# Seven block products of 256 columns in place of eight for twelve gate and up tile pairs of each layer

## The reference

```python
g_, u_ = jnp.split(h @ w_gate_up[i], 2, axis=-1)      # h: 512 x 1024, w_gate_up: 1024 x 5632
h2 = layer_norm(DEEPNORM_ALPHA * h + (jax.nn.silu(g_) * u_) @ w_down[i], ln2_g[i], ln2_b[i])
```

## Time and profile before

| | |
|---|---|
| median of three runs | 2374.94 us |
| the profiled execution | 2375.34 us |
| its span, first to last instruction | 2373.7 us |
| PE busy | 2340.2 us, 99% of the span |
| DVE, ACT, POOL busy | 1463.1, 1356.0, 460.5 us |
| moved by DMA | 402.79 MB, mean 170 GB/s |

### The profile page before, as it was taken

The page is one execution under the profiler, slowest core; times in us unless marked ns, Lnnn a source line. Parts: engine busy times, 40 slices in busy tenths (PEclk is TensorE's granted clock), DMA queues, the critical chain, the costliest instruction groups (busy, mean ns, idle before and its releaser), DMA issues.

```text
span 2373.7 us, 34430 instructions
## 1 busy us (share of the span) xinstructions
PE 2340.2 (99%) x11448; PEld 1936.3 (82%) x11448; DVE 1463.1 (62%) x2572; ACT 1356.0 (57%) x2239; POOL 460.5 (19%) x557
## 2 busy tenths in 40 slices
PE   8999999999999999999999999999999999999999
PEld 6878888887777888888788888888878778888886
DVE  4899898989545211113758999989895461111147
ACT  5756657376564554344757566664755655544446
POOL 2222222222111111111112122221211111111110
PEclk9999999999999999999999999999999999999999
DMA  7676575857888788888675857747578887888985
GB/s 206 142 168 152 124 175 120 185 127 162 181 180 201 167 194 191 192 209 187 162 157 121 184 127 162 175 109 171 132 176 179 185 187 179 192 191 196 213 186 139
DMA packets 112251, 402.79 MB, mean 170 GB/s; under 512 B 12400, under 2 KB 12400, under 8 KB 112112
## 3 DMA queue, kind: packets, MB, share of 16 engines
q0 software_dynamic: 54144, 195.06, 48.1%
q1 hardware_dynamic: 55728, 200.56, 26.1%
q10 hardware_dynamic: 2240, 5.42, 0.6%
HBM read 398.89 MB, written 2.10 MB: 169 GB/s over the span
## 4 chain that ended last, share of the span: by engine, by line
PE 81%; ACT 8%; DVE 6%; DMA 3%; issue 2%; DVEq 0%; SPq 0%; POOLq 0%; ACTq 0%
PE bank L882 22%; PE bank L884 22%; PE bank L883 22%; PE bank L924 3%; PE bank L925 3%; PE bank L927 3%; DMA w_lo<-w_stream 2%; ACT decay L515 2%; PE bank L1001 1%; ACT w_lo L464 1%; ACT w_hi L463 1%; PE bank L1007 1%; PE bank L1221 1%; DVE tmp_m L1403 1%; ACT y_hi L536 1%
## 5 line engine op out<-in xcount | busy, mean ns | idle before, releaser
L882 PE MATMUL bank<-x_hi,w_hi 128*128 128x512 f32 x1728 | 686.0, 397 | 0.1
L884 PE MATMUL bank<-x_hi,w_lo 128*128 128x512 f32 x1728 | 673.4, 390 | 0.0
L883 PE MATMUL bank<-x_lo,w_hi 128*128 128x512 f32 x1728 | 672.7, 389 | 0.0
L362 POOL DMA_DIRECT2D w_lo<-w_stream x376 | 323.3, 860 | 1654.7 <-ACT w_lo L464 1574.9
L463 ACT ACTIVATE w_hi<-w_raw 128x1024 fp32r<-128x1024 f32 (+1 forms) x378 | 400.3, 1059 | 281.5 <-PE bank L884 240.0
L464 ACT ACTIVATE w_lo<-w_raw 128x1024 fp32r<-128x1024 f32 (+1 forms) x378 | 397.6, 1052 | 0.0
L882 PEld LDWEIGHTS bank<-x_hi,w_hi 128*128 128x128 f32 x1728 | 324.6, 188 | 69.0 <-issue 3.7
L884 PEld LDWEIGHTS bank<-x_hi,w_lo 128*128 128x128 f32 x1728 | 324.4, 188 | 68.5
L883 PEld LDWEIGHTS bank<-x_lo,w_hi 128*128 128x128 f32 x1728 | 324.7, 188 | 68.0 <-issue 3.4
L1316 DVE SCALAR_TENSOR_TENSOR z_a<-glu_out,params,z_a 128x497 f32<-128x497 f32 (+14 forms) x480 | 320.8, 744 | 0.0
L1794 DVE TENSOR_TENSOR glu_out<-bank,sigmoids 128x512 f32<-128x512 f32 x44 | 30.4, 692 | 405.0 <-PE bank L884 405.0
(11 more groups left out here) (256 smaller groups left out, 3564.4 us busy)
## 6 DMA issues: line engine op xcount, KB each, us to landing
w_raw<-w_stream SPq DMA_DIRECT2D x362, 512.0 KB, 5.1
w_lo<-w_stream POOLq DMA_DIRECT2D x360, 512.0 KB, 7.7
w_raw<-w_stream SPq DMA_DIRECT2D x16, 384.0 KB, 3.7
w_lo<-w_stream POOLq DMA_DIRECT2D x16, 384.0 KB, 5.9
z_b<-x_in SPq DMA_DIRECT2D x4, 512.0 KB, 7.6
out<-z_b SPq DMA_DIRECT2D x4, 512.0 KB, 6.2
ple_p<-p_in ACTq DMA_DIRECT2D x2, 512.0 KB, 6.6
w_ple_in<-w_ple ACTq DMA_DIRECT2D x2, 512.0 KB, 12.4
```

The costliest lines, as they stand in the source:

```text
L362: gp.dma_start(wlo[:, s, 0:n], w_stream[cyc, s, :, 0:n].bitcast(F32R), accum_op=ALU.add).then_inc(lo_done[s], 16)
L882: pe.matmul(dst, wh, mh, start=first, stop=False)
L883: pe.matmul(dst, wh, ml, start=False, stop=False)
L884: return pe.matmul(dst, wl, mh, start=False, stop=last)
```

## The change

The first 4 of the 16 pairs of `C_UP0` and `C_UP1` stay as they were (`WHOLE`, two cycles). The other 12 of each layer become "units". In a unit the gate tile and the up tile are one 2x2 block matrix (rows: gate, up; columns: the lower and the upper half of the input features), and `h` is a 2x2 block matrix too (the two halves of the features by the two halves of the tokens). The product of the two has eight block products; the change forms it with seven (`P1` to `P7`) from sums and differences of blocks:

- four combinations of `h` (`combine`), made once per layer from `z_a` with its bias, split in high (ACT, `combined_hi`) and low (DVE, `combined_low`), each 128x1024;
- four combinations of the weights of each unit (`sums`: `S1` to `S4`, 128x512 each, on DVE), rounded by ACT (`sum_hi`), with the low part by DVE (`sum_low`);
- three products with plain weight blocks (`P1`, `P2`, `P4`), rounded by ACT from the staged tiles (`ringed`) and completed by POOL's adding DMA, 256 KB each, in a ring of four half slots;
- each product is 4 x 3 = 12 matmuls of 128x256 into one half bank; DVE puts the four output blocks together with seven additions of 256 columns (`out`, `finish`), ACT keeps `P1` and applies Silu to the gate in two halves.

The staged tiles of a unit come by two loads of 512 KB to `z_a` or `w_raw`, three units in turn. `z_a` is overwritten, so DVE adds `x_hi` and `x_lo` again behind the last unit. The additions of the bias to `z_a` move on ACT ahead of the first tile of the part. The core of the diff:

```diff
+RING_ORDER = [(0, "P1"), (0, "P2"), (0, "P4"), (1, "P1")]
+for _n in range(UNITS):
+    RING_ORDER += [(_n + 1, "P2"), (_n + 1, "P4"), (_n + 2, "P1")]
+RING_ORDER = [(_n, _p) for _n, _p in RING_ORDER if _n < UNITS]
...
+                for n in range(UNITS):
+                    j = n % STAGES
+                    if n >= STAGES:
+                        sp.wait_ge(s_sum, seen(4 * (UNITS * L + n - STAGES) + 4))
+                        sp.wait_ge(ring_done, seen(RINGED * L + ringed_until(n - STAGES, "P4")))
+                    elif j == 1:
+                        for s in (2, 3):
+                            sp.wait_ge(hi_done[s], seen(L * CYCLES + C_DOWN0))
+                    else:
+                        sp.wait_ge(t_done, seen(4 * (L + 1)))
+                    for t in range(2):
+                        w = w_units[L * UNITS + n, t]
+                        if j == 1:
...
-                for first, end, n in ((C_GATE_A, C_DOWN2, WT), (C_DOWN2, C_PLE, LAST * P), (C_PLE, CYCLES, WT)):
+                for first, end, n in ((C_GATE_A, C_DOWN0, WT), (C_DOWN0, C_DOWN2, WT), (C_DOWN2, C_PLE, LAST * P), (C_PLE, CYCLES, WT)):
+                    if first == C_DOWN0:
+                        for i, (u_, p) in enumerate(RING_ORDER):
+                            q = ring_place(u_, p) % SLOTS
+                            gp.wait_ge(ring_done, seen(RINGED * L + i + 1))
+                            settle(gp)
+                            t, h = {"P1": (1, 0), "P2": (1, 1), "P4": (0, 1)}[p]
+                            gp.dma_start(part(wlo, q), w_units[L * UNITS + u_, t, :, h * HALF:(h + 1) * HALF].bitcast(F32R),
+                                         accum_op=ALU.add).then_inc(ring_lo[q], 16)
                     with gp.Fori(first + (first == C_GATE_A), end) as c:
                         lo(base + c, 0, 1, 2, 3, n=n)
...
+                for m in range(KT):
+                    act.wait_ge(xl_done, seen(KT * k + m + 1))
+                    act.activation(za[:, m, :], za[:, m, :], ACT.Identity,
+                                   bias=par[:, O_LN1 + KT + m:O_LN1 + KT + m + 1]).then_inc(zf_ready, 1)
...
+                    j, c = n % STAGES, ring_place(n, p)
+                    act.wait_ge(unit_loaded[j][0 if p == "P4" else 1], 16 * (UNITS // STAGES * L + n // STAGES + 1))
+                    if c >= SLOTS:
+                        after(*ring_owner(c - SLOTS))
+                    w = staged(n, {"P1": 2, "P2": 3, "P4": 1}[p])
+                    act.activation(part(whi, c % SLOTS), w, ACT.Copy)
+                    act.activation(part(wlo, c % SLOTS), w, ACT.Copy, scale=-1.0).then_inc(ring_done, 1)
+
...
+                def frame(n):
+
+                    if n > 0:
+                        gate_columns(n - 1, 1, g2_done)
+                    if n < UNITS:
+                        sum_hi(n, "S4")
+                        after(n, "P1")
+                        act.wait_ge(fl_done, seen(FT * L + WHOLE + n - 1))
+                        act.activation(u[:, n % 2, 0:HT], bank[product_bank(n, "P1")][:, 0:HT], ACT.Copy).then_inc(kept, 1)
+                        if n < UNITS - 1:
+                            ringed(n + 1, "P2")
+                            ringed(n + 1, "P4")
+                        else:
+                            hi(on(post, C_DOWN0), 0)
+                        sum_hi(n, "S3")
+                    if n > 0:
+                        unit_hi(n - 1)
+                    if n < UNITS:
+                        gate_columns(n, 0, g1_done)
+                        ringed(n + 2, "P1")
+                    if n < UNITS - 1:
+                        sum_hi(n + 1, "S1")
+                        sum_hi(n + 1, "S2")
+                    elif n == UNITS - 1:
+                        after(n, "P4")
+                        hi(on(post, C_DOWN0), 1)
+                        after(n, "P5")
+                        hi(on(post, C_DOWN0), 2)
+                        after(n, "P7")
+                        hi(on(post, C_DOWN0), 3)
+
+                for i in range(4):
+                    combined_hi(i)
+                for f in range(WHOLE):
+                    r = f % 2
+                    c = on(post, C_UP0 + f // 2)
+                    last = f >= WHOLE - 2
+                    take(c, 2 * r, sg[:, :], ACT.Silu)
+                    if not last:
+                        hi(on(c, 1), 2 * r)
+                    elif r == 1:
+                        sum_hi(0, "S1")
+                        sum_hi(0, "S2")
+                    act.wait_ge(evac[2 * r + 1], seen(c[1] + 1))
+                    act.activation(aah[:, f, :], u[:, r, :], ACT.Copy).then_inc(fh_done, 1)
+                    if not last:
+                        hi(on(c, 1), 2 * r + 1)
+                    elif r == 0:
+                        ringed(0, "P1")
+                        ringed(0, "P2")
+                        ringed(0, "P4")
...
+                for n in range(UNITS + 1):
+                    frame(n)
...
-                swiglu(on(post, C_UP0), KT, aah)
-                for m in range(KT):
-                    act.wait_ge(xl_done, seen(KT * k + m + 1))
-                    act.activation(za[:, m, :], za[:, m, :], ACT.Identity,
-                                   bias=par[:, O_LN1 + KT + m:O_LN1 + KT + m + 1]).then_inc(zf_ready, 1)
-                swiglu(on(post, C_UP1), KT, abh)
...
+                        mh, ml = xh[:, a:a + 4, t:t + HT], xl[:, a:a + 4, t:t + HT]
+                    else:
+                        i = {"P5": 0, "P6": 1, "P7": 2, "P4": 3}[p]
+                        mh, ml = combined(i, 0), combined(i, 1)
+                    wh, wl = part(whi, q), part(wlo, q)
+                    for k_ in range(4):
+                        w = slice(k_ * P, (k_ + 1) * P)
+                        i = three(bank[product_bank(n, p)][:, 0:HT], wh[:, w], wl[:, w], mh[:, k_, :], ml[:, k_, :],
+                                  k_ == 0, k_ == 3)
...
+                for n in range(UNITS):
+                    for p in ORDER:
+                        product(n, p)
...
                 dve.wait_ge(zf_ready, seen(2 * KT * (L + 1)))
-                settle(dve)
+                combine(0, quadrant(0, 1), quadrant(0, 0))
+                dve.wait_ge(t_ready, seen(4 * L + 1))
+                combine(1, quadrant(1, 1), combined_sum(0))
+                combine(2, quadrant(1, 1), quadrant(0, 1))
+                dve.wait_ge(t_ready, seen(4 * L + 2))
+                combine(3, quadrant(1, 0), combined_sum(1))
+                for i in range(4):
+                    combined_low(i)
...
+                            for t in range(2):
+                                dve.wait_ge(unit_loaded[n % STAGES][t], 16 * (UNITS // STAGES * L + n // STAGES + 1))
+                            a, b, op = staged(n, 0), staged(n, 1), ALU.add
+                        elif name == "S2":
+                            dve.wait_ge(s_sum, seen(count + 1))
+                            a, b, op = part(wsum, S_BUF["S1"]), staged(n, 2), ALU.subtract
+                        elif name == "S4":
+                            dve.wait_ge(s_sum, seen(count + 2))
+                            a, b, op = staged(n, 3), part(wsum, S_BUF["S2"]), ALU.subtract
+                        else:
+                            a, b, op = staged(n, 2), staged(n, 0), ALU.subtract
+                        dve.tensor_tensor(part(wsum, S_BUF[name]), a, b, op).then_inc(s_sum, 1)
...
+                for n in range(UNITS + 1):
+                    if n > 0:
+                        finish(n - 1)
+                    if 0 < n < UNITS:
+                        sums(n, "S3")
+                    if n < UNITS:
+                        sum_low(n, "S2")
+                    if n > 0:
+                        gated(n - 1)
+                    if n < UNITS:
+                        un, gn = u[:, n % 2, :], gate_of[n % 2]
+                        dve.wait_ge(kept, seen(U0 + n + 1))
+                        out(n, "C11", gn[:, 0:HT], un[:, 0:HT], "P2")
+                        sum_low(n, "S4")
+                    if n > 0:
+                        low_act(WHOLE + n - 1)
+                    if n < UNITS:
+                        out(n, "b", un[:, 0:HT], un[:, 0:HT], "P6")
+                        sum_low(n, "S3")
+                        out(n, "c", un[:, HT:T], un[:, 0:HT], "P5", "b")
+                        if n < UNITS - 1:
+                            sums(n + 1, "S1", "S2")
+                        out(n, "C12", gn[:, HT:T], un[:, HT:T], "P3", "c")
+                        if n < UNITS - 1:
+                            sums(n + 1, "S4")
+                            sum_low(n + 1, "S1")
+                dve.wait_ge(ring_done, seen(RINGED * (L + 1)))
+                for m in range(KT):
+                    step(dve.tensor_tensor(za[:, m, :], xh[:, m, :].bitcast(F32), xl[:, m, :].bitcast(F32), ALU.add))
+                dve.wait_ge(dve_order, issued())
+                restart()
```

(55 more changed lines are left out.)

150 lines of the change are left out of this document (143 added, 7 removed).

## The result

The changed kernel takes 2384.03 us (median of 12 executions, 2377.64 to 2388.58), the kernel before 2375.57 us on the same chip (12 executions, 2373.74 to 2378.87). The ratio is 1.0031, 95% interval 1.0023 to 1.0039: slower by 8 us in 2400, while PE has less to do. The forecast was 2383.3 us. The profiled execution of the changed kernel took 2385.37 us, its span is 2383.5 us (before: 2373.7), so the two traces differ by 9.8 us, a little more than the medians do.

What follows compares the result with a forecast made beforehand. PE, busy for 99% of the span, was taken to bound the kernel. The terms -19.4 + 18.8 + 4.2 + 4.8 = +8.4 us on the profiled 2375.3 gave 2383.7, as a median 2383.3 us; range 2370 to 2397.

Steps and rivals of the forecast that it cites:

- Part 1: Units on PE: 84 matmuls of 256 columns at 119.9 ns, 10.07 us for a pair's 10.88; 24 units give -19.4 us.
- rival C: Units: the 13 ns per matmul don't apply to one-piece operands of 256 columns; 26.6 us less, 2357; chance 0.06.
- Part 2: Other engines inside units: all beneath PE's 10.07 us, DVE near 8.4; landings up to 7.6 us hidden; cost nothing.
- Part 3: Entry, once per layer: additions and combinations delay slot 0 of the second cycle; PE waits 9.4 us more, +18.8 us total.
- Rival A: Entry: with less traffic POOL's DMA lands in 6.6 us and the clock stays up; not slower, 2373.6 us; chance 0.23.
- Part 4: Clock behind the entry wait: falls to half rate, costing 2.1 us per layer, +4.2 us; bounds 0 to 2.1.
- Part 5: Exit, once per layer: slot 0 of `C_DOWN0` is rounded behind the last unit's `P1`; PE waits 2.4 us, +4.8 total.
- Rival B: Units: DVE's 17 instructions don't overlap and become the bound, 10.6 us a unit, +12 us more, 2395; chance 0.17.

Runs made afterwards that it cites:

- The two DVE kernels: Changed kernel plus two, or four, unused 512-column additions on DVE in every unit: 2380.62 and 2415.84 us.
- The filled gap: Changed kernel plus 35 unused 512-column matmuls per layer ahead of the second up cycle, where PE waits: 2378.82 us.
- entry moved: Changed kernel with bias additions and all combine work moved behind the second whole tile pair, in each layer: 2377.84 us.
- both ends changed: Changed kernel with combinations moved behind the second whole pair and the first down slot rounded and fetched in halves: 2360.16 us.
- the last kernel: Changed kernel with combinations moved, bias additions split, exit in halves, and unit loads into `z_a` released by the last combination: 2354.74 us, ratio 0.9916.

## Why the prediction was right

**Part 1** held: -19.4 was forecast, 24 x (10.88 - 10.07) is what the trace shows, and 20.3 us were left when the waits were gone. The price of 120 ns, taken from matmuls with a two-piece operand, holds for one piece; rival C is out. So are the 9.2 us a unit that would follow, as an estimate, from N/2.4 + 2.5 ns, which the Trainium skill states for back-to-back matmuls ("TensorE: Matmul & The Clock Gate", "Wait — 56ns, not 53.3ns?"); in the section that the forecast names, the back-to-back issue gap, the same formula is that of a single matmul. The trace has 119.9 ns where it gives 109.

**Part 2** held: no wait in the units and DVE below PE. Its 8.4 us are not what its own terms give, 10 x 0.58 + 7 x 0.416 = 8.7, unless the additions of 256 columns overlap as well. A unit in the middle has 8.61 us of DVE work; the 8.39 above are a mean over twelve, of which the first has less. The landing was right too, 5.3 us for 256 KB, between the 4 and 6 expected and under the 7.6 that are hidden:

```profile
w_lo<-w_units POOLq DMA_DIRECT2D x72, 256.0 KB, 5.3
```

The two DVE kernels show that this was no near miss.

**Part 3** had the right chain and was 1.4 and 0.9 us too large: 9.4 forecast, 8.0 and 8.5 measured. The delay was right: the take came 9.64 us later, of which 0.4 are PE's own, whose rows there are all later by that much (796.50 for 796.08). The term that was mis-sized is the landing, taken as long as before, 8.33 us, and measured at 7.19 and, in layer 1, 7.51. Rival A had named a shorter landing, for less traffic; that traffic is the reason was not tested.

**Part 4** had the right sign and was a little small: 2.1 a layer forecast, 2.6 and 3.0 measured, since the slow stretch lasted 5.4 us in layer 0 (805.00 to 810.43) and 6.2 in layer 1 (1988.66 to 1994.86), where the first rows of the program had 4.3. The filled gap shows that it is paid: 5.2 us by the medians and 3.3 by the ratios, for 4.2 forecast. The rule that an idle array falls back to half rate ("TensorE: Matmul & The Clock Gate" of the Trainium skill, the HAM clock gate) agrees with this trace: 0.43 us per 512 columns behind 8.5 us of idle time.

**Part 5** had the right place and size for the wait, 2.4 a layer against 2.3 and 1.9. It missed a term: the clock falls behind a gap as short as this as well, 1.7 us in layer 0. Part 4 had ruled that out from a gap near 2.4 us in the trace of before, and that was a misreading. The one gap of that length, 2.43 us (9.14 to the 11.57 of the earlier trace rows), stands at the start of the program, where 512 columns take 0.43 us on both sides of it, so it can't show that the clock stays up. The longest at full clock is 2.17 us:

```profile
9.14 0.63 PE L884 MATMUL bank<-x_hi,w_dt_lo 128*64 128x512 f32 x1
...
672.06 0.39 PE L884 MATMUL bank<-x_hi,w_lo 128*128 128x512 f32 x1
674.23 0.47 PE L882 MATMUL bank<-act_a_hi,w_hi 128*128 128x512 f32 x1 [1.78 <-DVE act_a_lo L1459]
```

The sum was +8.4; the account of the trace gives +8.7, with an entry smaller by 2.3 and clock terms larger by 3.2 than forecast. That the total came within 1 us is in part this cancelling, and in part luck: the executions of the changed kernel lie 11 us apart. **Rival A** (entry mostly covered) failed on its condition: the wait was over 7 us and the clock fell. **Rival B** failed as shown.

## What to carry to other kernels

A saving inside a stretch where one engine is always busy is real, and safe as long as the others stay below it; look for the price at its two ends, where the preparation of the new scheme stands ahead of work that was just in time. Move such preparation behind the takes that feed the busy engine, and then ask what waits for the preparation: moved whole, the 8 us reappeared at the next place; moved in the right pieces, and with each load released by the last reader of its buffer only, they vanished. Count a wait of PE at more than its length, for it may also cost the clock.

## What the runs showed of the hardware

**A gap of 2 to 3 us can cost the clock, and needn't.** In the changed kernel and its variants 11 gaps at the entry and the exit, from start to start, lie between 2.14 and 3.49 us. Eight of them (2.14, 2.32, 2.41, 2.48, 2.54, 2.82, 3.12, 3.49) were followed by half clock, which cost 1.7 to 1.8 us each; three (2.31, 2.77, 3.11) were not. Four of 1.6 to 2.1 us there were not either. The ten gaps of 7.6 to 8.8 us, at the entry or where it was moved to, all were. Elsewhere it goes both ways as well: of the gaps at the matmul of the row at 674.23 and its like in layer 1, two of 2.17 us and one of 2.30 left the clock up, one of 2.19 and one of 2.42 (entry moved, gap filled) didn't, and the two of 2.04 us in unit 0 with four more additions on DVE were followed by half clock. One kernel can go either way from one execution to the next: with both ends changed, the mean clock was 0.997 in one execution of the four and 1.000 in two, 8 us apart in time. The changed kernel spreads by 11 us in 12 executions; the last kernel by 2.6 us in 5, but the kernel before, at a mean clock of 0.997 to 1.000, by 6.6 us in 31, so the clock is not all of it.

**The clock can fall after PE has resumed.** Behind the exit gap of layer 0 four matmuls follow each other at 0.23 to 0.31 us, and only then they take 0.40 and 0.43.

**The 13 ns beside the columns exist at the full clock only.** With the entry moved whole, the first products of unit 0 run at half clock:

```profile
827.78 0.41 PE L1095 MATMUL bank<-x_hi,w_hi 128*128 128x256 f32 x1
...
832.69 0.41 PE L1097 MATMUL bank<-h_combined_b,w_lo 128*128 128x256 f32 x1
```

Those are 23 steps in 4.91 us, 213.5 ns each, and 256 columns at 1.2 GHz are 213.3. At the full clock the same products take 119.9 for 106.7. The Trainium skill says the same of kind ("TensorE: Matmul & The Clock Gate", "Wait — 56ns, not 53.3ns?": exact while cold, a fixed cost once warm) and gives 2.5 ns for it; the traces here have 13. What sets it was not tried.

**Adding DMAs of the same size, 512 KB, took 7.2 to 9.2 us to land at the entry.** The transfer of slot 0 there took 8.33 us before, 7.19 and 7.51 after, and slot 1's took 9.23 with the gap filled; the earlier trace rows have 6.6 to 9.3. Where PE waits for a landing, this term was good to about a microsecond and no better in these traces.
